# Even mixer of a four-stage network: a causal filter run as 32-column tiles between the projections

## The reference, cut to what matters

```python
def even_mixer(h, w_in, w_out, conv_w, conv_b, ln_g, ln_b, q_g, k_g, sinks):
    a_val, a_gate, q, k, v = jnp.split(h @ w_in, cuts, axis=-1)      # 512, 512, 512, 128, 128
    u = a_val * jax.nn.sigmoid(a_gate)
    # causal depthwise convolution of u: 31 taps, 512 channels
    u = lax.conv_general_dilated(u, conv_w[:, None, :], (1,), ((30, 0),), ...) + conv_b
    u = jax.nn.silu(layer_norm(u, ln_g, ln_b))
    q, k = rms_norm(q, q_g), rms_norm(k, k_g)                        # per head of 64
    o = banded_attention(q, k, v, 127, sinks)                        # 8 query heads, 2 key heads
    return jnp.concatenate([u, o], axis=-1) @ w_out
```

## Time and profile before

| | |
|---|---|
| time, median of 3 runs | 1788.22 us (1786.56 to 1789.99) |
| the profiled execution | 1788.19 us |
| its span, first to last instruction | 1786.4 us |
| PE busy | 1770.4 us, 99% |
| DVE busy | 1272.3 us, 71% |
| ACT busy | 948.3 us, 53% |
| the even mixer, from its norm to the next one's | 190.01 to 298.79 us of the span |

### The profile page before, as it was taken

How to read it: one execution, slowest core, us unless ns; L and a number is a source line. 1 busy time by engine, 2 the same in 40 slices (tenths; PEclk the granted TensorE clock), 3 DMA queues, 4 the chain that set the end, 5 groups by cost and what they waited for, 6 DMA issues and landing times.

```text
span 1786.4 us, 24851 instructions
## 1 busy us (share of the span) xinstructions
PE 1770.4 (99%) x9682; PEld 1506.9 (84%) x9682; DVE 1272.3 (71%) x1913; ACT 948.3 (53%) x1348; POOL 30.4 (2%) x40
## 2 busy tenths in 40 slices
PE   9999999999999999999999999999999999999998
PEld 8888888888888888888888788888888878888887
DVE  7774895876577657677656977777756878677774
ACT  6554655555455546555545535455545544555553
POOL 0000000000000001000000000000000000000000
PEclk9999999999999999999999999999999999999999
DMA  8666523666666655366655544556665454466663
GB/s 267 199 178 202 177 72 118 189 178 201 180 195 185 194 175 185 113 196 185 196 173 180 180 129 131 177 180 189 190 196 172 140 155 127 151 187 193 188 195 109
DMA packets 227679, 309.25 MB, mean 173 GB/s; under 512 B 22559, under 2 KB 176319, under 8 KB 227563
## 3 DMA queue, kind: packets, MB, share of 16 engines
q1 hardware_dynamic: 227398, 307.35, 56.3%
q10 hardware_dynamic: 164, 0.30, 0.1%
HBM read 306.57 MB, written 1.05 MB: 172 GB/s over the span
## 4 chain that ended last, share of the span: by engine, by line
PE 92%; DVE 5%; ACT 2%; issue 1%; DMA 0%; SPq 0%; POOLq 0%; POOL 0%; ACTq 0%; DVEq 0%
PE ps L649 26%; PE ps L598 15%; PE ps L600 15%; PE ps L599 15%; PE ps L651 13%; DVE wlo L1744 1%; PE ps L1148 1%; PE ps L610 1%; PE ps L820 1%; PE ps L846 1%; DVE ev_acc L1753 1%; ACT whi L1246 1%; PE ps L833 1%; PE ps L788 0%; DVE m_scr L1753 0%
## 5 line engine op out<-in xcount | busy, mean ns | idle before, releaser
L1744 DVE TENSOR_TENSOR wlo<-staging,whi 128x1024 fp32r<-128x1024 f32 (+1 forms) x580 | 692.7, 1211 | 335.8 <-ACT whi L1246 335.5
L1246 ACT ACTIVATE whi<-staging 128x1024 fp32r<-128x1024 f32 (+1 forms) x580 | 606.2, 1050 | 473.3 <-PE ps L600 293.6
L649 PE MATMUL ps<-hT,whi 128*128 128x512 f32 x1984 | 623.5, 396 | 0.0
L651 PEld LDWEIGHTS ps<-hT,wlo 128*128 128x128 f32 x1984 | 372.7, 188 | 88.1
L651 PE MATMUL ps<-hT,wlo 128*128 128x256 f32 x1984 | 389.9, 278 | 0.0
L649 PEld LDWEIGHTS ps<-hT,whi 128*128 128x128 f32 x1984 | 302.1, 189 | 0.0
L598 PE MATMUL ps<-whi,fh 128*128 128x512 f32 x504 | 196.1, 389 | 0.0
L599 PE MATMUL ps<-wlo,fh 128*128 128x512 f32 x504 | 196.1, 389 | 0.0
L600 PE MATMUL ps<-whi,fl 128*128 128x512 f32 x504 | 196.1, 389 | 0.0
L598 PE MATMUL ps<-whi,hT 128*128 128x512 f32 (+3 forms) x464 | 184.6, 398 | 0.8 <-DVE wlo L1744 0.6
L600 PE MATMUL ps<-whi,hT 128*128 128x512 f32 (+3 forms) x464 | 177.4, 382 | 0.0
(11 more groups left out here) (351 smaller groups left out, 1906.7 us busy)
## 6 DMA issues: line engine op xcount, KB each, us to landing
staging<-in_w_in SPq DMA_DIRECT2D x92, 512.0 KB, 3.4
staging<-in_ffn_w_gate SPq DMA_DIRECT2D x84, 512.0 KB, 4.3
staging<-in_ffn_w_up SPq DMA_DIRECT2D x84, 512.0 KB, 4.5
staging<-in_ffn_w_down SPq DMA_DIRECT2D x84, 512.0 KB, 4.2
staging<-in_w_ffn_gate SPq DMA_DIRECT2D x44, 512.0 KB, 4.3
staging<-in_w_ffn_up SPq DMA_DIRECT2D x44, 512.0 KB, 4.6
staging<-in_w_ffn_down SPq DMA_DIRECT2D x44, 512.0 KB, 4.2
staging<-in_od_w_in SPq DMA_DIRECT2D x16, 512.0 KB, 3.7
```

Of the source, the lines that this page charges most:

```text
L649: e.matmul(o, wh[:, kk, j * 128:j * 128 + 128], hT[:, k, :], start=k == 0, stop=False)
L651: m = e.matmul(o[:, 0:256], wl[:, kk, j * 128:j * 128 + 128], hTh[:, k, :], start=False, stop=k == KD - 1)
L1246: e.activation(high(u)[:, 0:n], stage[u % NS][:, 0:n], ACT.Copy).then_inc(*K.inc("hi", ("hi", u)))
L1744: e.tensor_tensor(low_of(u)[:, 0:n], stage[u % NS][:, 0:n], high(u)[:, 0:n].bitcast(F32), ALU.subtract).then_inc(*K.inc("lo", ("lo", u)))
```

## The change

The filter becomes PE work alone. The taps are padded to 32 and taken four at a time: the contraction over 128 partitions is 32 channels times four neighbouring shifts, and a step k of eight moves the input by four. So `u4[32 s + c, j, q]` holds channel `32 q + c` of block j, shifted by s, and `w4` the weights as 128 x 32 matrices. The four quarters q of a block write 32 partitions each of one bank. To lay out `u4`, SP writes `u` to DRAM and reads it back with four shifts. The weights are transposed, halved, regrouped by 16 small transfers and spread by DVE in the first FFN. DVE adds only the bias. ACT's diagonals go.

The order changes as well: all values and gates are projected first, then q, k and v; `conv` runs in rounds 11 to 16, `swa` from 15 on PE and DVE and 14 on ACT (attention turns in rounds 19 to 29), `layer_norm` from 18, `down` from 24; and the filter's four row blocks of `w_out` come before the attention's.

```diff
-PE_TAPS = 11
+GROUPS = 4
+STEPS = 8
...
+        shift = nc.dram_tensor("ev_shift", (4, 128, PAD + S), F32, kind="Internal").ap()
...
                 plan_cols(ev, c, 256)
                 plan_cols(ev, 512 + c, 256)
-                if c == 0:
-                    plan_cols(ev, 1024, 512)
-                    plan_cols(ev, 1536, 256)
-            for r in (512, 768, 0, 256):
+            plan_cols(ev, 1024, 512)
+            plan_cols(ev, 1536, 256)
+            for r in (0, 256, 512, 768):
...
+                self.rows = [(self.mh[:, k, :], self.ml[:, k, :], ("ev ml",)) for k in range(4)]
+                self.rows += [(self.mh[:, 4 + k, :], self.ml[:, 4 + k, :], ("swa oT", k // 2))
+                              for k in range(4)]
...
+                    if f is f0 and p == 7:
+                        conv_weights(evs)
...
+                def conv():
+                    e.wait_ge(*K.at("ev w4"))
                     for j0 in (0, 2):
                         ps = room(("ev tap", j0))
...
+                        e.wait_ge(*K.at("ev u4", j0))
+                        for n in range(2 * STEPS):
+                            j, k = j0 + n // STEPS, n % STEPS
+                            c = 256 * (n // STEPS)
+                            for q in range(GROUPS):
+                                w = e.matmul(ps[32 * q:32 * q + 32, c:c + 256], m.w4[:, q, j, k, :],
+                                             m.u4[:, j, q, 4 * k:4 * k + S], start=k == 0, stop=k == STEPS - 1)
+                            if n + 1 == 2 * STEPS:
+                                w.then_inc(*K.inc("tap_mm", ("ev tap mm", j0)))
+                            if n + 1 in (6, 11, 16):
+                                yield
                         done("ev tap", j0)
...
-                weave([(1, products()), (11, swa()), (27, down(g, m.rows)), (24, layer_norm())])
+                weave([(1, products()), (11, conv()), (15, swa()), (24, down(g, m.rows)), (18, layer_norm())])
...
-                weave([(1, products()), (10, swa()), (6, diagonals()), (27, down(m.rows)), (24, layer_norm())],
-                      catch_up)
+                weave([(1, products()), (14, swa()), (24, down(m.rows)), (18, layer_norm())], catch_up)
...
+                def four_taps(m, q):
...
+                    e.tensor_tensor(m.w4[:, q, :, :, :].rearrange("p j k c -> p (j k) c"),
+                                    C("fold").unsqueeze(1).broadcast_to([128, 32, 32]),
+                                    m.wv[:, q, :, :].rearrange("p j k -> p (j k)").unsqueeze(2).broadcast_to(
+                                        [128, 32, 32]), ALU.mult).then_inc(
+                        *K.inc("ev_cw", *([("ev w4",)] if q + 1 == GROUPS else [])))
...
+                    if f is f0 and k in (8, 10, 12, 14):
+                        four_taps(evs, k // 2 - 4)
...
+                            e.tensor_scalar(m.acc[:, j, :], bk("ev tap", j0)[:, c:c + 256], m.cb[:, j, 0:1], None,
+                                            ALU.add).then_inc(
...
-                weave([(11, swa()), (1, products()), (5, conv()), (27, down(g, m.rows, 1.0)), (24, layer_norm())],
+                weave([(1, products()), (15, swa()), (14, conv()), (24, down(g, m.rows, 1.0)), (18, layer_norm())],
                       catch_up)
...
+            def taps_load(m, k):
+                e.wait_ge(*K.at("ev taps"))
+                load("ev_wv", *[(m.wv[quarters[k], q, :, :], m.cwt[quarters[q], k, :, :]) for q in range(GROUPS)],
+                     steps=[("ev wv",)] if k + 1 == GROUPS else [])
+
+            def shifted_load(m, j0):
+                e.wait_ge(*K.at("ev pad"))
+                e.wait_ge(*K.at("ev u", j0 + 1))
+                n = S + 4 * (STEPS - 1)
+                load(f"ev_shift_{j0}", (shift[j0:j0 + 2].rearrange("j p s -> p j s"), m.u[:, j0:j0 + 2, :]),
+                     steps=[("ev shift", j0)])
+                e.wait_ge(*K.at("ev shift", j0))
+                load(f"ev_u4_{j0}", *[(m.u4[quarters[k], j0:j0 + 2, :, 0:n].rearrange("c j q s -> c (j q) s"),
+                                       shift[j0:j0 + 2, :, 1 + k:1 + k + n].rearrange("j (q c) s -> c (j q) s", q=GROUPS))
+                                      for k in range(GROUPS)], steps=[("ev u4", j0)])
...
+            before = {first[1] + 10: (even_load, evs), first[0] + 30: (filter_load, evs),
+                      **{first[0] + 44 + k: (taps_load, evs, k) for k in range(GROUPS)},
+                      first[1] + 14: (shifted_load, evs, 0), first[1] + 18: (shifted_load, evs, 2), first[4] + 10: (odd_load, ods),
```

More of the change, by code:

```diff
@@ L778, in ffn, with conv_weights @@
                         done("dn", g, t, n)
+            def conv_weights(m):
+                ps = room(("ev cw",))
+                e.wait_ge(*K.at("ev no tap"))
+                e.wait_ge(*K.at("ev cwr"))
+                for j in range(4):
+                    w = e.transpose(ps[:, j * 35:(j + 1) * 35], m.cwr[:, j * 128:(j + 1) * 128], ident[0:35, 0:35])
+                w.then_inc(*K.inc("hT", ("ev cw mm",)))
+                done("ev cw")
             def heads_T(P, d, H, src):
@@ L861, in products @@
                         yield from tiles(g, [b[:, 0:256] for b in ps], 256, 4)
-                        second = tiles(g, [b[:, 256:512] for b in ps], 256, 4, [("ev u mm", j0)])
-                        next(second)
+                        gates = tiles(g, [b[:, 256:512] for b in ps], 256, 4, [("ev u mm", j0)])
+                        next(gates)
                         yield
-                        next(second)
+                        next(gates)
                         if not j0:
                             row(g)
-                        yield
@@ L869, in products @@
                         for j in range(2):
                             done("ev u", j0 + j)
[L871 to L877, removed]
+                        yield
+                    yield from x_cols(g, 0, 512)
+                    yield from x_cols(g, 512, 256)
@@ L893, in products @@
-                        done("ev tap", j0)
[L895 to L901, removed]
+                        e.wait_ge(*K.at("ev u4", j0))
[8 more added lines that the diff above has]
+                            if n + 1 in (6, 11, 16):
+                                yield
@@ L1415, in products @@
                             e.activation(th, th, ACT.Tanh, scale=0.5).then_inc(*K.inc("ev_tanh", ("ev tanh", j0 + j)))
[L1416 to L1431, removed]
-                            if last:
-                                yield
+                    yield from x_cols(512)
+                    by_token(g, 0, 512, lambda t: m.qkv[:, t, 0:512].rearrange("p (i j e) -> p j i e", i=4, j=2),
+                             src=lambda ps: ps.rearrange("p (j i e) -> p j i e", j=2, i=4))
+                    yield from x_cols(256)
+                    by_token(g, 512, 256, lambda t: m.qkv[:, t, 512:768])
                 def layer_norm():
@@ L1441, in layer_norm @@
                     for j in range(4):
-                        e.activation(m.sq[:, j, :], m.acc[:, j, :], ACT.Silu, scale=m.cw[:, j, 32:33],
-                                     bias=m.cw[:, j, 33:34]).then_inc(*K.inc("ln_silu"))
+                        e.activation(m.sq[:, j, :], m.acc[:, j, :], ACT.Silu, scale=m.cb[:, j, 1:2],
+                                     bias=m.cb[:, j, 2:3]).then_inc(*K.inc("ln_silu"))
                     e.wait_ge(*K.now("ln_silu"))
@@ L2078, in conv_weights @@
                                     ALU.mult).then_inc(*K.inc("ev_cw", ("ev less sinks",)))
+                    yield from x_cols(512)
+                    yield from x_cols(256)
                 def conv():
-                    e.wait_ge(*K.at("ev ch"))
-                    e.wait_ge(*K.at("ev pad"))
-                    def add_first(j0):
+                    for j0 in (0, 2):
+                        if j0:
+                            yield
+                            yield
+                            yield
@@ L2719, in sync_program @@
                 if u in before:
-                    stage_load, m = before[u]
-                    stage_load(m)
+                    stage_load, *m = before[u]
+                    stage_load(*m)
                 unit(u)
```

74 lines of the change are left out of this document (30 added, 44 removed).

## The result

The changed kernel takes 1792.85 us (median of six runs, 1791.98 to 1795.0), the kernel before 1787.4 in the same series (1786.56 to 1789.99). The ratio is 1.0029, 95% interval 1.0019 to 1.0039: slower, by about 5 us. The forecast was 1790.5, 2.3 above the 1788.2 that it started from, with a range of 1784 to 1805, and slower was its likeliest side.

A forecast was written before the change was run, and what follows sets the result against it. TensorE, busy 99% of the span, was taken to bound the kernel. Taps -4.0 us, then late norm, starvation and low clock, summed to +1.9, plus 0.4 for weights' transposes: +2.3 on 1788.2, so 1790.5 us, range 1784 to 1805.

The forecast's parts named there:

- two at a time: Rival for the filter's column tiles: only two run together, or partly; +13.7 us, 1804.2 us at two; chance 0.18.
- one at a time: Rival for the filter's column tiles: they run one after another; +41.3 us, 1831.8 us; chance 0.14.
- Taps: Filter on PE: -18.9 + 13.7 + 1.2 = -4.0 us, four tiles at once; projections and taps end at 247.1.
- Removed work at nothing: Even mixer: 76 DVE tap steps (36.3 us), 4 first ones and 44 ACT diagonals removed, costed at no gain.
- Transfers hidden: Filter input's DRAM round trip hidden by 5 us or more, second half over 10; late-transfers rival 1795.5 us, chance 0.04.
- (1): Before the attention: q's norm starts late, at 242.2; keys scaled 248.2, bias adds 249.1, mean's matmuls end at 250.9.
- (2): Layer norm chain after the mean: centre and square to 253.4, variance products 255.2, root and diagonals 256.7.
- (3): Attention starts only in round 19: first exponentials 255.6, turns about 1.9 us each, rs product behind turn 3 at 259.6.
- (4): Filter's rows: copy, normalise, silu, rounding to 264.5; ACT's turn 4 queues behind the silu, its exponentials done at 267.1.
- Starvation: PE short of work around the layer norm and first attention turns: 9 us in all, against 2.9 before.
- (5) Clock: Emptier stretch from 251 to 267 puts turns 1 to 5 and first half row at 1.2 GHz, to 271.5.
- The faster rival: Attention starves PE no more than before, near 2.9 us instead of 9: 6.1 us go, 1784.4; faster side 0.13.

The follow-up runs named there:

- tiles in turn: Changed kernel with the same 128 filter products ordered tile by tile instead of one step of each of the four tiles; 1823.89 us, one run.
- old order: Column tiles alone, with projections, attention and output product in the order of the kernel before; 1789.88 us, ratio 1.0016 to the kernel before.
- mixed order: Against the old order, filter inputs 2 and 3 projected before the keys, filter steps still beside the attention turns; 1783.69 us, ratio 0.9980 to the kernel before.
- fill: Changed kernel plus twelve products nobody reads, placed in TensorE's three longest attention waits; 1789.81 us, ratio 1.0012 to the kernel before.
- late queries: Mixed order but with the changed kernel's projection order: both halves of filter inputs, then queries, then keys and values; 1785.68 us, ratio 0.9979 to the kernel before.

## Why the prediction was right, and where its sizes were off

Its side, its median within 0.13% and its mechanism held: the tiles run four at once, and the order takes that back by starvation and clock. The size of the change did not hold: +2.3 us was forecast, and the medians differ by 5.4. Of the 3.1 missing, 1.1 lie in the mixer (steps 1 to 5 below) and 0.35 ahead of it; the other 1.7 are between the profiled executions and the medians, before's 0.8 above its median and after's 0.9 below. That the time itself came so near owes something to luck: the start of 1788.2 was 0.8 above the later median of before. And two terms missed in opposite directions, the starvation too high and the clock too low.

Step by step, after's times less the 0.74 us by which it came late to the mixer:

- **Taps**: said 247.1 for the end of projections and filter, measured 247.13. Four at once was right, and the two rivals (two at a time, one at a time) were wrong; tiles in turn shows what one at a time would be. The trip was taken at 0.3, measured 0.35 between the full-size products. The Trainium skill ("TensorE: Matmul & The Clock Gate", Part 3: Packing small matmuls) gives 2.38 times for three column tiles; here four ran four times as fast as one, since a step of four takes the 0.43 of a single product. The Trainium skill says that a change of tiling mode drains the engine ("TensorEngine Tiling (Array Packing)", Key Properties); the traces show a price that agrees, 0.35 us for a trip beside the 128-row products and only 0.14 beside the attention's own small shapes.
- **Removed work at nothing**: right to within 2 us, by the run without VectorE's steps; ScalarE's diagonals no run tests.
- **Transfers hidden**: right here, with 4.3 us to spare for the first pair and 6.2 for the second (5 and over 10 were said), and right only in this order, by the 4.8 us of the old order.
- **(1), (2)**: keys scaled 248.3 (said 248.2), bias sums 249.1 (249.1), square 253.6 (253.4), variance 255.6 (255.2), diagonals 257.1 (256.7). The POOL roots that carry (1):

```profile
244.73 2.90 POOL L2580 TENSOR_TENSOR ev_hr<-ev_hr,phalf 128x16 f32<-128x16 f32 x1 [46.14 <-DVE ev_hr L1975]
247.60 1.01 POOL L2580 TENSOR_TENSOR ev_hk<-ev_hk,phalf 128x4 f32<-128x4 f32 x1
```

- **(3), (4)**: DVE took the rs product at 260.3 (said 259.6), because turns 2 and 3 and that product itself, 1.22 us, ran at 1.2 GHz; I had priced the product at nothing. The 0.7 runs through: rounding 265.2 (264.5), turn 4's exponentials 267.8 (267.1), first half row's end 272.3 (271.5).
- **Starvation**: said 9 us, too high; measured 6.8 (2.92, 1.85, 1.17, 0.44, 0.27, 0.15), against 2.9 before. The holes stand where the walk put them; PE's half-speed work filled part of them.
- **(5) Clock**: this is the mis-sized term. It ran at 1.2 GHz from 256.8 to 273.9 and not from 251 to 271.5, 17.1 us in all. With turn 6's parts at half speed the stage ended at 301.8 where I had 300.7. By the fill, what lies behind 267 costs about 2 us of the stretch's 3.1.
- The other runs of after are 0.8 to 3.0 us above the profiled one, with mean clocks of 0.992 and 0.993 against 0.994. 0.001 of 1791 us at half speed is 3.6 us more of low clock. Where these lie no profile shows; the forecast's "one or two more slow windows" is their size.

The stretch by terms: taps -4.0, transposes moved out -0.5, starvation +3.9 (6.8 against 2.9), together -0.6. The measured +3.14 leaves 3.7 for the clock: 13.7 us more at 1.2 GHz than before, 4.1 of them idle, and half of the other 9.6 is 4.8 at most. The fill shows 2 of this directly; the rest is argued, not shown.

The faster rival (the attention starves PE no more than before) failed here and came true in the mixed order: with filter steps left between the turns, waits fell to 2.1 us, the clock held in the profiled execution, and 3.5 of the tiles' 4 us arrived in the median. **What costs the changed kernel its gain is thus the order: the filter ahead of the attention and the norm's chain beside the turns that this leaves bare.** No run moves one of the two alone. The layer norm's chain and the turns want the same ScalarE, and no TensorE work was left to stand between them.

## What to carry to other kernels

Work of the busiest engine that looks like the thing to shrink may be the cover of a latency-bound chain beside it: shrink it, but leave what remains between the chain's links, a few steps per link, and not in a block ahead of it. The layer norm moved with the filter in the runs behind this. A trip through DRAM wants its inputs made early, so move the projection, not the consumer. When a function's table change and a long activation stand in the queue of the engine that paces a chain, moving them by one link moves the wait with them.

## What the runs showed of the hardware

- Four float32 matmuls of 128 x 32 weights with four different moving operands, in four column tiles, start 6 to 7 ns apart and take together the 0.432 us of one. In tile order, PE begins the next tile's products up to four records ahead of the last tile's end, and no earlier.
- The granted clock fell to 1.2 GHz at 256.8 in the fill, where PE's records left 0.65 of the 7.8 us before it uncovered. What stood there were transposes, 64-row scores and products of one moving column (16 records in 1.9 us) beside 1.8 us of filling (251.74 to 253.57), and the longest wait was 0.44. Covering the waits did not keep it up in this execution, though in one of ten the mean clock was 1.000. The profiled executions of the mixed order and of late queries, with filter steps between the turns, have 0 us of low clock in the stretch.
- With bare attention turns the clock stood at 1.2 GHz for 37.5 us on end, a loss of up to 15.7 us, against 13.6 us of named waits in that whole mixer.
